# Scores of the rotated part on all 128 rows, grouped identity products, and a new written order of both mixers' calls

## What is computed

```python
def first_block(x, ...):                      # two layers
        x = x + 0.5 * swiglu(rmsnorm(x, ...), ...)
        x = x + hybrid_mixer(rmsnorm(x, ...), ...)
        x = x + 0.5 * swiglu(rmsnorm(x, ...), ...)

def hybrid_mixer(...):                        # the first mixer
    proj = h @ w_in
    (qa, ka, va, qi, ki, wi, qb, kb, vb, qc, kc, vc, ga, gb, gc) = jnp.split(proj, offsets, axis=-1)
    ...
    o_a = dsa_attention(qa, ka, va, qi, ki, wi)   # keys chosen by an indexer and a top-k
    o_b = moba_attention(qb, kb, vb)
    o_c = diff_attention(qc, kc, vc, ...)
    ...

def second_block(x, ...):                     # two layers
        h = h + 0.5 * swiglu_2(rms_norm(h, ...), ...)
        u = rms_norm(h, ...)
        z, xbc, dt_raw, cq, ckv, kr, gates = split_cols(u @ w_in[l], IN_SPLIT_SIZES)
        y_ssd = ssd_branch(z, xbc, dt_raw, ...)   # a scan in two chunks of 128 tokens
        y_mla = mla_branch(cq, ckv, kr, ...)      # 8 heads: 128 plain and 64 rotated columns
        ...
def mla_branch(...):
    ...
    q = jnp.concatenate([q[..., :128], apply_rope(q[..., 128:], cos, sin)], axis=-1)
    k = jnp.concatenate([k[..., :128], apply_rope(k[..., 128:], cos, sin)], axis=-1)
    o = causal_block_attention(q, k, v)
```

## Time and profile before

| | |
|---|---|
| runs shown | 2814.66, 2816.95, 2819.82 us; median 2816.95 |
| the profiled execution's time | 2815.74 us |
| its span in the profile | 2813.8 us |
| mean granted TensorE clock | 0.993 |
| busy share of the span | TensorE 98%, weight loads 91%, VectorE 64%, ScalarE 51%, POOL 10% |

### The profile page before, as it was taken

How to read it: one execution, slowest core, us unless ns; L and a number is a source line. 1 busy time by engine, 2 the same in 40 slices (tenths; PEclk the granted TensorE clock), 3 DMA queues, 4 the chain that set the end, 5 groups by cost and what they waited for, 6 DMA issues and landing times.

```text
span 2813.8 us, 48877 instructions
## 1 busy us (share of the span) xinstructions
PE 2762.2 (98%) x20056; PEld 2572.7 (91%) x20056; DVE 1791.9 (64%) x3060; ACT 1433.7 (51%) x2441; POOL 283.7 (10%) x442
## 2 busy tenths in 40 slices
PE   9998999999998999999999999999999999999999
PEld 8998999999998999999998799999999978899998
DVE  6557857456567857556458787564564686875654
ACT  5445645445445645445446575454444565754543
POOL 0003311000003311000002212100000021111000
PEclk9999999999999999999999999999999999999999
DMA  5552354545543354445444234544444442344443
GB/s 207 191 193 106 121 179 170 192 183 181 191 164 107 134 180 182 180 169 191 180 170 165 77 135 150 181 181 180 185 175 181 184 150 88 123 165 180 165 185 145
DMA packets 64732, 462.02 MB, mean 164 GB/s; under 512 B 7296, under 2 KB 7808, under 8 KB 9344
## 3 DMA queue, kind: packets, MB, share of 16 engines
q1 hardware_dynamic: 64512, 458.90, 44.3%
HBM read 457.83 MB, written 1.05 MB: 163 GB/s over the span
## 4 chain that ended last, share of the span: by engine, by line
PE 86%; DVE 8%; ACT 2%; POOL 2%; issue 1%; DMA 1%; SPq 0%; DVEq 0%; POOLq 0%; ACTq 0%
PE bank L456 17%; PE bank L378 17%; PE bank L380 17%; PE bank L379 17%; PE bank L389 3%; PE bank L391 3%; PE bank L390 3%; PE bank L644 2%; DVE WLO L2340 2%; POOL MTA L3499 1%; PE bank L1084 1%; PE bank L422 1%; DMA RAW<-weights_dram 1%; ACT PBA L1650 1%; PE bank L1008 1%
## 5 line engine op out<-in xcount | busy, mean ns | idle before, releaser
L2340 DVE TENSOR_TENSOR WLO<-RAW,WHI 128x1024 fp32r<-128x1024 f32 (+1 forms) x872 | 1059.4, 1253 | 296.2 <-ACT WHI L1436 295.5
L1436 ACT CAST WHI<-RAW 128x1024 fp32r<-128x1024 f32 (+1 forms) x872 | 886.0, 1047 | 374.5 <-DMA RAW<-weights_dram 228.9
L378 PE MATMUL bank<-XH,WHI 128*128 128x256 f32 x3712 | 1060.7, 286 | 3.7 <-DVE WLO L2340 3.7
L380 PE MATMUL bank<-XH,WLO 128*128 128x256 f32 x3712 | 1051.4, 283 | 0.0
L379 PE MATMUL bank<-XL,WHI 128*128 128x256 f32 x3712 | 1051.3, 283 | 0.0
L378 PEld LDWEIGHTS bank<-XH,WHI 128*128 128x128 f32 x3712 | 712.5, 192 | 11.2 <-issue 3.1
L379 PEld LDWEIGHTS bank<-XL,WHI 128*128 128x128 f32 x3712 | 712.6, 192 | 5.5
L380 PEld LDWEIGHTS bank<-XH,WLO 128*128 128x128 f32 x3712 | 712.7, 192 | 0.0
L1500 ACT ACTIVATE SG<-bank 128x256 f32<-128x256 f32 x152 | 58.5, 385 | 484.9 <-PE bank L380 484.9
L2453 DVE TENSOR_TENSOR HF<-SG,bank 128x256 f32<-128x256 f32 x152 | 63.9, 420 | 340.0 <-ACT SG L1500 340.0
L389 PE MATMUL bank<-WHI,XH 128*128 128x256 f32 (+2 forms) x928 | 269.4, 290 | 4.3 <-DVE XL L2394 3.4
(11 more groups left out here) (341 smaller groups left out, 3187.9 us busy)
## 6 DMA issues: line engine op xcount, KB each, us to landing
RAW<-weights_dram SPq DMA_DIRECT2D x431, 1024.0 KB, 4.8
RAW<-weights_dram SPq DMA_DIRECT2D x2, 800.0 KB, 4.2
X<-x_dram SPq DMA_DIRECT2D x2, 512.0 KB, 5.4
RAW<-weights_dram SPq DMA_DIRECT2D x2, 512.0 KB, 6.1
out_dram<-X SPq DMA_DIRECT2D x2, 512.0 KB, 2.7
RAW<-weights_dram SPq DMA_DIRECT2D x2, 384.0 KB, 3.2
CM<-mixer_dram SPq DMA_DIRECT2D x2, 320.5 KB, 9.6
CM<-mixer_dram SPq DMA_DIRECT2D x2, 176.0 KB, 5.3
```

Source lines behind the costliest of these rows:

```text
L378: self.e.matmul(bank, h, xh[:, x0 + k, :], start=k == k0, stop=False)
L380: ins = self.e.matmul(bank, l, xh[:, x0 + k, :], start=False, stop=k == k1)
L1436: e.copy(WHI[:, c % NHI, a:b], RAW[:, c % NLO, a:b]).then_inc(*up("hi", c, p))
L2340: e.tensor_tensor(WLO[:, c % NLO, a:b], RAW[:, c % NLO, a:b], WHI[:, c % NHI, a:b].bitcast(F32), ALU.subtract).then_inc(*up("lo", c, p))
```

## The change

**Scores.** The rotated part's product runs on all 128 rows. KP keeps the even heads in rows 0 to 63 with zeros below; a new tile KPB has the odd heads in rows 64 to 127 with zeros above. A new POOL call `blank2` clears both once per layer, and `kpt` is two copies of 64 partitions that wait for it. KPB takes space of XSB and RT2, so `xs_` for j = 2 waits for the scores of unit 5 (before, j = 0 waited for the rotated queries), and a scratch tile moves to PBB.

**yp.** The four identity products of a second chunk stand together in front of the eight products of 64 columns.

**Order.** The lists of both mixers are in a new order on all four engines.

```diff
@@ msc @@
             for k, h in enumerate(hs):
-                rows = slice(64 * (h % 2), 64 * (h % 2) + 64)
                 o = ps[:, k * nk:k * nk + nk]
                 e.matmul(o, QN[:, h, qs], KN[:, h, 0:nk], start=True, stop=False)
-                e.matmul(o, QP[rows, h // 2, qs], KP[rows, h // 2, 0:nk], start=False, stop=False)
+                e.matmul(o, QP[:, h // 2, qs], (KP, KPB)[h % 2][:, h // 2, 0:nk], start=False, stop=False)
@@ yp @@
             if c == 1:
                 e.wait_ge(*at("yo", n, g))
+                yo = JUNK[:, M2_SQUARE.index[("yo", g)] % 2, :]
+                for b in range(4):
+                    col = (b % 2) * 256 + P
+                    e.matmul(PS[2 + b // 2][:, col:col + P], yo[:, b * P:b * P + P], IDN, start=b % 2 == 0, stop=False)
             for b in range(4):
                 ps = PS[2 + b // 2]
                 col = (b % 2) * 256 + c * P
-                if c == 1:
-                    e.matmul(ps[:, col:col + P], JUNK[:, M2_SQUARE.index[("yo", g)] % 2, b * P:b * P + P], IDN, start=True, stop=False)
                 for h in range(2):
                     hh = 2 * b + h
-                    ins = e.matmul(ps[64 * h:64 * h + 64, col:col + P], XDT[:, c, hh * 64:hh * 64 + 64], LE[:, c, hh * P:hh * P + P], start=c == 0, stop=True)
+                    ins = e.matmul(ps[64 * h:64 * h + 64, col:col + P], XDT[:, c, hh * 64:hh * 64 + 64], LE[:, c, hh * P:hh * P + P], start=c == 0, stop=c == 0 or b % 2 == 1)
@@ kpt @@
             e.wait_ge(*at("qtr", n, "kp", t))
-            e.copy(KP[:, 0:4, t * P:t * P + P], PS[7][:, :].rearrange("p (a q) -> p a q", q=P)).then_inc(*up("kpt", n, t))
+            e.wait_ge(*at("blank", n))
+            ps = PS[7][:, :].rearrange("p (a q) -> p a q", q=P)
+            e.copy(KP[0:64, 0:4, t * P:t * P + P], ps[0:64])
+            e.copy(KPB[64:P, 0:4, t * P:t * P + P], ps[64:P]).then_inc(*up("kpt", n, t))
@@ POOL @@
+        def blank2(self, n):
+
+            e.wait_ge(*at("tr", n, 1, 3))
+            e.memset(KP[:, :, :], 0.0)
+            e.memset(KPB[:, :, :], 0.0).then_inc(*up("blank", n))
@@ TensorE, m1 @@
             self.at_(n, 3, 1, 1)
+            self.at_(n, 4, 0, 0)
+            self.at_(n, 4, 0, 1)
+            self.at_(n, 4, 1, 0)
             self.ptr(n, 2)
-            self.at_(n, 4, 0, 0)
+            self.at_(n, 4, 1, 1)
             self.ix(n, 0, 0)
...
+            self.sc(n, 0, 0)
+            self.sc(n, 0, 1)
+            self.at_(n, 6, 1, 1)
+            self.at_(n, 7, 0, 0)
+            self.at_(n, 7, 0, 1)
+            self.at_(n, 7, 1, 0)
+            self.at_(n, 7, 1, 1)
             self.ptr(n, 4)
-            self.at_(n, 6, 1, 0)
-            self.at_(n, 6, 1, 1)
             self.ptr(n, 5)
@@ TensorE, m2 @@
             self.ktr(n, 0, 0)
+            self.ktr(n, 0, 1)
             self.bk(n, 1, 1, 0)
-            self.ktr(n, 0, 1)
             self.bk(n, 1, 1, 1)
             self.bx(n, 0, 0, 0)
             self.bx(n, 0, 0, 1)
+            self.kptr(n, 0)
             self.bx(n, 0, 1, 0)
+            self.ktr(n, 1, 0)
             self.bx(n, 0, 1, 1)
+            self.ktr(n, 1, 1)
             self.bx(n, 1, 0, 0)
-            self.kptr(n, 0)
             self.bx(n, 1, 0, 1)
-            self.ktr(n, 1, 0)
+            self.kptr(n, 1)
             self.bx(n, 1, 1, 0)
-            self.ktr(n, 1, 1)
-            self.bx(n, 1, 1, 1)
-            self.kptr(n, 1)
-            self.bz(n, 0, 0, 0)
             self.msc(n, 0)
             self.msc(n, 1)
+            self.bx(n, 1, 1, 1)
+            self.bz(n, 0, 0, 0)
```

More of the change, by code:

```diff
@@ L250, in build @@
     KP = sb("KP", [P, 4, 256], F32, at_kb(20))
+    KPB = sb("KPB", [P, 4, 256], F32, at_kb(88.5))
     VM = sb("VM", [P, 2, D], F32, at_kb(24))
@@ L661, in m1 @@
             self.tr(n, 1, 1)
+            self.at_(n, 2, 0, 0)
             self.tr(n, 1, 2)
             self.tr(n, 1, 3)
-            self.at_(n, 2, 0, 0)
             self.at_(n, 2, 0, 1)
@@ L697, in m1 @@
             self.at_(n, 6, 0, 1)
+            self.at_(n, 6, 1, 0)
+            self.sc(n, 0, 0)
[5 more added lines that the diff above has]
+            self.at_(n, 7, 1, 1)
             self.ptr(n, 4)
-            self.at_(n, 6, 1, 0)
-            self.at_(n, 6, 1, 1)
             self.ptr(n, 5)
@@ L706, in m1 @@
             self.sc(n, 2, 0)
-            self.at_(n, 7, 0, 0)
+            self.ptr(n, 7)
+            self.at_(n, 8, 0, 0)
             self.sc(n, 3, 0)
@@ L712, in m1 @@
             self.pv(n, 1)
[L713 to L718, removed]
             self.at_(n, 8, 0, 1)
             self.at_(n, 8, 1, 0)
+            self.pt(n, 2)
             self.at_(n, 8, 1, 1)
+            self.pv(n, 2)
+            self.at_(n, 9, 0, 0)
+            self.at_(n, 9, 0, 1)
+            self.at_(n, 9, 1, 0)
+            self.at_(n, 9, 1, 1)
+            self.ptr(n, 8)
+            self.at_(n, 10, 0, 0)
+            self.at_(n, 10, 0, 1)
+            self.at_(n, 10, 1, 0)
+            self.at_(n, 10, 1, 1)
             self.pt(n, 3)
-            self.ptr(n, 7)
-            self.at_(n, 9, 0, 0)
+            self.ptr(n, 9)
+            self.at_(n, 11, 0, 0)
             self.pv(n, 3)
-            self.at_(n, 9, 0, 1)
+            self.at_(n, 11, 0, 1)
             self.pt(n, 4)
-            self.at_(n, 9, 1, 0)
+            self.at_(n, 11, 1, 0)
             self.pv(n, 4)
-            self.at_(n, 9, 1, 1)
-            self.at_(n, 10, 0, 0)
+            self.at_(n, 11, 1, 1)
             self.pt(n, 5)
-            self.ptr(n, 8)
-            self.at_(n, 10, 0, 1)
+            self.ptr(n, 10)
+            self.at_(n, 12, 0, 0)
             self.pv(n, 5)
[L736 to L746, removed]
             self.sc(n, 6, 0)
@@ L749, in m1 @@
             self.sc(n, 7, 0)
+            self.at_(n, 12, 0, 1)
+            self.at_(n, 12, 1, 0)
+            self.sc(n, 7, 1)
+            self.sc(n, 8, 0)
+            self.pt(n, 6)
             self.at_(n, 12, 1, 1)
             self.ag(n, 0, 0, 0)
-            self.sc(n, 7, 1)
-            self.pt(n, 6)
-            self.sc(n, 8, 0)
+            self.sc(n, 8, 1)
             self.pv(n, 6)
-            self.ag(n, 0, 0, 1)
-            self.sc(n, 8, 1)
             self.sc(n, 9, 0)
             self.pt(n, 7)
-            self.ag(n, 0, 1, 0)
+            self.ag(n, 0, 0, 1)
             self.pv(n, 7)
@@ L2745, in m1 @@
             self.lo(c + 6, 0)
+            self.pss(n, 3)
             self.lo(c + 6, 1)
-            self.pss(n, 3)
+            self.lo(c + 7, 0)
+            self.lo(c + 7, 1)
             self.acc(n, 0, 0)
@@ L2922, in xs_ @@
             e = self.e
[L2923 to L2924 removed]
+            if j == 2:
+                e.wait_ge(*at("sc", n, 5))
             for i in range(2):
```

466 lines of the change are left out of this document (230 added, 236 removed).

## The result

The changed kernel takes 2792.34 us, median of four runs (2787.12 to 2792.77), against 2816.7 for the kernel before: a ratio of 0.9908, 95% interval 0.9891 to 0.9925. The forecast was 2793. The total is nearly exact, and that is the smaller part of what there is to learn: the sum lacks a term of about 10 us, and others in it came out too large, so that the errors cancelled. The profiled run took 2792.47, with a span of 2790.7.

A forecast was written before the change was run, and what follows sets the result against it. TensorE, busy 98% of the span, was taken to bound the kernel. 2815.74 − 9.3 − 8.4 − 6 − 0 = 2792.0, and as the profiled run lies 1.2 under the median, 2793 us; range 2787 to 2799.

The forecast's parts named there:

- Scores, 9.3: Second mixer's scores: the rotated product on all rows saves 0.29 us per head, 32 heads, 9.3 us; bounds 7.4 to 9.9.
- yp, 8.4: Second chunk's yp calls: grouped identity products take 2.00 us instead of 3.05, 8.4 us over 4 groups in 2 layers.
- Rival D: Second mixer's scores: their gain is swallowed as TensorE waits for the softmax instead; 2802 us, chance 0.05.
- First mixer's order, 6: First mixer: TensorE's waits fall from 6.5 to about 4.3 us per layer, with less half clock; 3 per layer, 6 us.
- the half clock at 234: First mixer: 3.41 us at 0.50 clock after the idling at ptr 2, costing 1.7 us; expected gone in the changed profile.
- Second mixer's order, 0: Second mixer: 2.6 us wait at kptr(1) goes, 2.4 to 3.4 comes, so 0; −2 to +2 per layer.
- rival B: Both mixers: only the changes of shape pay, the new order moves waits without shrinking them; 2799 to 2805 us, chance 0.20.
- the likeliest case: Whole kernel: the forecast itself, 2793 us with its own range of 2787 to 2799, chance 0.60.
- C: First mixer: the reordering takes nearly all of its wait, 2 × 8.2 in place of 6; 2783 us, chance 0.08.
- E: Scores and yp: pauses come not from shape but something that stays; 2810 us, or 2802 where only yp saves; chance 0.03.
- F: Scores: weight loads on all rows stop TensorE, costing 12.2 us, and the 9.3 is not saved; 2814.5 us, chance 0.02.
- G: Second mixer: TensorE stands at kptr(0) for POOL, about 15 us per layer; slower, 2823 us, chance 0.02.

The follow-up runs named there:

- half_rows: The changed kernel with the scores' rotated product on 64 rows again, nothing else: 2800.61 us.
- yp_mixed: The changed kernel with a second chunk's four identity products between the 64-column products again, nothing else: 2795.56 us.
- old_lists: The changed kernel with all lists of both mixers in the old order; shapes, places and clears as in the change: 2792.89 us.
- lo_later: The changed kernel with one wait added: the second mixer's five VectorE lo calls behind rk(1) start after POOL's kp(0): 2781.92 us, ratio 0.9876.
- places_old: The changed kernel with the work area starting where the kernel before had it, nothing else: 2803.34 us.

## Why the prediction was right, and where it was not

The total of 2793 and the range held, by luck in the sum. By the prediction's own steps:

- **Scores, 9.3.** The 0.29 per head is 0.29 and 0.30 in the trace, 9.4 in TensorE's instructions; undone alone it costs 8.3 in time by the medians and 9.2 in the second-mixer phases of the profiles. Right. The Trainium skill, "TensorEngine Tiling (Array Packing)", "Key Properties", says that a change of tiling mode drains TensorE; the pitch in the earlier trace rows and its return in half_rows agree with that.
- **yp, 8.4.** 3.05 became 2.01, 8.3 in instructions. In time it is less sure: 3.2 by yp_mixed, and both changes of shape with the old order gave 14.5 of 17.7. Rival D, which was given the scores alone and 0.05, holds as a remainder of about 3 us, as waits for VectorE and ScalarE (old_lists).
- **First mixer's order, 6.** Right only in kind: three waits became one, and the half clock at 234 is gone. The order is worth 3.4, and the two things that the term adds up did not give it. The waits named went from 6.5 to 5.25 per layer instead of 4.3, because the term took pss(7)'s small second instruction at its length elsewhere, 0.17, and it took 0.87 beside POOL; TensorE idles only 1.5 us less in both layers together, where the forecast had 4.4. The half clock only moved behind the one wait: 17 us before and 17 after. The forecast counted the stretch at 234 and left out those that the kernel before had at ptr 5. Most of the gain is in TensorE's busy time, for which the term has nothing; from which products it comes was not traced.
- **Second mixer's order, 0.** The step that failed. It took kp(0)'s time as fixed by POOL's unchanged list and so a wait of 2.4 to 3.4 at kptr(0); it was 4.9 and 5.5, as kp(0) came 1.8 and 2.6 us later after the chain's start than before. POOL's list up to there is the same, but its small instructions are long while VectorE's lo calls run, and in the new order of VectorE, where lo(c + 14, 1) stands behind rk(1) instead of in front of it, more of them meet a lo. lo_later shows that the lo calls are what makes kp(0) late. What the new order costs in time, 2.9 us by the medians, lies within the bounds given and is not told from nothing.
- **Places, not in the sum at all.** The change's part on buffers was read as housekeeping and got no term and no rival. It is worth 9.6 to 11 us, as much as the scores.

Without the places the forecast would have been compared with about 2802 to 2803 (places_old, 2803.34): inside the range, but there as rival B's 2799 to 2805, the case that had 0.20. So the likeliest case was hit by a gain it did not know of, which by the medians stood in for 3 us of the shapes, 2.6 of the first mixer's order and 2.9 of the second's.

Rivals: B came true in part (the order as a whole gave about 0.5), C no, E and F no (half_rows), G's mechanism yes, at 5 us per layer instead of 15. The price of F had a weak place: it took the halves of the kernel before to alternate, but all heads of a unit lie in the same half (M2_UNITS), so they did not alternate there either.

## What to carry to other kernels

Price every line of a diff, the moved buffers too: run the change's places alone in the old kernel, since it costs one run and here was 40% of the gain. When an order moves work next to other work on VectorE and POOL, take durations from rows where both run, not from rows where one is idle. And a long wait is often best removed at what makes its releaser late, even by adding a wait elsewhere.

## What was not expected of the hardware

- The pitch of 512-column products depended on where the operand that is not the weights lay, within 160 bytes: feed-forward phases of 190.47, 190.03, 189.48 and 189.29 us for 160, 128, 64 and 0 bytes short of the weights' place in 1024. Like products in the same runs, with XL, which did not move, stayed at 389 to 390 ns each.
- POOL's instructions on 8 columns took 1.02 to 1.09 us beside VectorE's lo calls and mostly 0.20 to 0.27 without; one of VectorE's took 1.13 beside a POOL instruction on 512 columns and 0.17 without. The Trainium skill, "SBUF — State Buffer", "Who interferes with whom", says that VectorE and GpSimd share one pair of ports, held as an exclusive lock, and that a VectorE instruction with two SBUF inputs (lo is one) contends with a GpSimd instruction that reads SBUF. The traces agree, in both directions.
- Behind single waits of about 5 us TensorE's clock was granted at about half: 0.55 over 6.8 us and 0.56 over 9.5 in the first mixers (269.00 and 891.50), 0.50 over 3.4 in the second mixer (1553.90). Joining three waits into one left the first mixers' time at half clock at 17 us.
